# Mixture-of-experts layers of a transformer kernel: ranked groups, each expert fetched once, the smallest group at 64 rows

## The chip, the cores and the metric

The kernel runs on one core of one Trainium2 chip. The metric is the device time of one execution in microseconds. The numbers are fp32: every weight tile is split on the chip into a high part and a low part (both fp32r), and a product x·w is computed as xh·wh + xl·wh + xh·wl, three matmuls for one.

## The reference, cut to what matters

The whole model is four layers over 256 tokens of width 1024. The change touches only the two mixture-of-experts layers, one after each of the first two mixers:

```python
def hier_moe(x, wr_g, br_g, wr_e, br_e, w_gate, w_up, w_down):
    ...
    g_logits = (xt @ wr_g + br_g).astype(f32)
    _, g_idx = lax.top_k(g_logits, 1)                 # 1 of 4 groups for each token
    ...
    top_v, top_i = lax.top_k(e_logits, MOE_TOP_K)     # 2 of that group's 4 experts
    e_w = jax.nn.softmax(top_v, axis=-1) * g_w[:, None]
    ...
        h = jax.nn.silu(xc @ wg) * (xc @ wu)          # 16 experts, 1024 -> 512
        h = (h.reshape(-1, N_EXPERTS, EXPERT_HIDDEN) * gc[..., None])...
        return h @ wd                                 # 512 -> 1024, summed over the experts
```

Each token uses two experts, both of its own group. So 256 tokens fall into four groups, and a group's experts need only the group's tokens.

## The kernel before, in words

Each engine runs its own program, written out in Python in the order in which it is to run; semaphores tie them together (`wait_ge(signal, name)` waits until the instruction that carries that name has ended). The engines in the expert stage (class `Moe`) do this:

- **SP** fetches tiles of 128x1024 fp32 (512 KB) in the order of `MOE_TILES` into a ring of ten (`rawb`, `experts`). A tile's place is fetched anew when its low part has been made.
- **ACT** (`Scalar.split_half`, profile line 522) copies a tile to its high part, **DVE or POOL** (`Low.split_half`, line 549: raw minus high) makes the low part. The field `lo` in `stream_order` says which of the two. There are five places for split tiles; `fed()` stands at the point where a tile has been used and splits the tile that takes its place, so the lead over TensorE is at most five tiles.
- **PE** (matmuls line 608, transposes line 624) works in *units*. A unit is one expert for one block of up to 128 gathered tokens: eight gate-and-up tiles, six matmuls of 512 columns each (`pe_first`); silu on ACT, the product with the gate on DVE (`scalar_tensor_tensor`, line 105), four transposes (`pe_turn`), the transposed h split by ACT and DVE (`hid`); four down tiles, six matmuls each (`pe_down`).

The tokens of each group are gathered to one block with one-hot matmuls (`pe_gather`, matrix `P`): blocks 0 to 3. Tokens beyond 128 in a group go to a fifth block. That makes `UNITS = 19`: 16 units, whose tiles have fixed addresses, and three more for the fifth block, whose experts are chosen at run time (`dve_chosen` writes `S.chosen`, SP reads it with `value_load`, line 483). SP fetches the first ten tiles of a layer before the routing is known. A block's four units add up in PSUM (`yb`), and the block is split and scattered back with one-hot matmuls (`pe_combine`, `pe_place_last`). The order is a fixed pipeline, `steps(UNITS, 2)`: gate-and-up of unit u, then down of unit u-1. POOL makes the low parts of the first four tiles of a layer, DVE all others.

Of the kernel before, what the change touches and what calls it, by code (L numbers as in the profile page):

```python
# [8 lines left out]
F32 = mybir.dt.float32  # L9
# [14 lines left out]
EXPERT_ROOM = 1024 * XRAW + 2560  # L24
# [184 lines left out]
def stream_order(dram):  # L209
# [67 lines left out]
UNITS = 19  # L277
MOE_TILES = [(("gu", "d")[k], u, i) for k, u in steps(UNITS, 2) for i in range((8, 4)[k])]
# [27 lines left out]
class Shared:  # L306


    def __init__(self, nc, ctx, dram, out):
# [6 lines left out]
        self.hrow_ = sb("hrow", 2048)  # L316
        hH = sb("hH", 2048, F32R)
# [14 lines left out]
        self.chosen = sb("chosen", 3, U32)[:, :]  # L332
# [119 lines left out]
class Sync(Lane):  # L452
# [8 lines left out]
    def program(self, S):  # L461
        chosen = None
# [3 lines left out]
        for n, (src, _, lo, ring) in enumerate(S.order):  # L466
            if ring in ("moe0", "moe1") and S.order[n - 1][3] != ring:
                self.wait_ge(S.product, "rows", 2 * int(ring[3]))
                chosen = None
# [6 lines left out]
            if ring in ("moe0", "moe1"):  # L476
                name, layer, unit, k, step = src
                if unit < 16:
                    src = S.dram[name][layer, step * unit + k]
                else:  # L480
                    if chosen is None:
                        self.wait_ge(S.vdone, "moe.chosen", layer)
                        chosen = [self.eng.value_load(S.chosen[0:1, i:i + 1], min_val=0, max_val=15)
                                  for i in range(3)]
                    src = S.dram[name][layer, bass.ds(chosen[unit - 16] * step + k, 1)].rearrange("a p f -> p (a f)")
# [1458 lines left out]
class Moe:  # L1944
# [3 lines left out]
    def __init__(self, S, layer, norm):  # L1948
        self.S, self.layer, self.norm = S, layer, norm
        R = Room(S.experts_r, 2048 * XSPLIT)  # L1950
        self.xr = R.get(5, 2048)
        rows = R.get(2, 2, 1024)
        self.rH, self.rL = rows[:, 0, :, :], rows[:, 1, :, :]
        self.P = R.get(2, 640)
        self.PT = R.get(1280)
        self.tri, self.all, self.hot = self.PT[:, 256:384], self.PT[:, 384:512], self.PT[:, 512:532]
        self.pair = self.PT[:, 544:576].rearrange("p (a g e) -> p a g e", a=2, g=4)
        self.g2 = self.PT[:, 1040:1056].rearrange("p (a f) -> p a f", a=2)
        R = Room(S.experts, 1024 * XRAW)
        self.s = [R.get(512) for _ in range(2)]  # L1960
        self.h = [R.get(512) for _ in range(2)]
# [17 lines left out]
        self.first = R.get(2)  # L1979
        self.e1 = R.get(2, 4)  # L1980
        self.e2 = R.get(2, 4)
        self.seldom_e = R.get(4)
        self.turned = R.get(3)
        self.past = R.get(3)
        self.take = R.get(3, 4)
        self.at = R.get(1)
        self.pos = R.get(2, 4)
        self.over = R.get(2)
        self.full = R.get(5)
# [4 lines left out]
        self.gate = R.get(20)  # L1994
        self.hT = [S.hid[:, 1024 * i:1024 * i + 1024] for i in range(2)]
# [5 lines left out]
    def x_stat(self, b, k):  # L2001
        return self.xr[:, b, 128 * k:128 * k + 128], self.xr[:, b, 1024 + 128 * k:1152 + 128 * k]

    def pe(self, pe):
        S, n = self.S, self.layer
        pe.rows_T = ("hT", self.norm)
        self.pe_route(pe)
        self.pe_count(pe)
        self.pe_gather(pe)
        yb = tb = None  # L2010
        for u in range(UNITS + 1):
            if u == 0:
                for k in range(8):
                    self.pe_first(pe, 0, k, k + 1)
                    if 1 <= k < 5:
                        self.pe_gather_over(pe, (k - 1) // 2 * 4, (k - 1) % 2)
                    elif k == 5:
                        self.pe_gates(pe)
                        self.pe_turn_hot(pe, 0)
                    elif k == 6:  # L2020
                        self.pe_turn_hot(pe, 1)
                        self.pe_turn_hot(pe, 2)
            elif u < UNITS:
                self.pe_first(pe, u, 0, 4)
                self.pe_turn(pe, u - 1, tb)
                self.pe_first(pe, u, 4, 8)
            else:
                self.pe_combine(pe, 1, range(4))
                self.pe_turn(pe, u - 1, tb)
                self.pe_combine(pe, 0, range(4))  # L2030
            if u == 0:
                yb = [pe.open("moe.y", n, i) for i in range(2)]
                tb = [pe.open("moe.T", n, i) for i in range(2)]
            elif u < UNITS:
                self.pe_down(pe, u - 1, yb)
        self.pe_down_last(pe, yb)
        for half in range(2):
            self.pe_place_last(pe, half)
# [28 lines left out]
    def pe_count(self, pe):  # L2067
# [9 lines left out]
        pe.busy(b, 4)  # L2077
# [6 lines left out]
    def pe_gather(self, pe):  # L2084
        S, n = self.S, self.layer
        for k in range(8):
            for part, r in ((0, self.rH), (1, self.rL)):
                b = pe.open("moe.g", n, k, part)
                if k + part == 0:
                    pe.busy(b, 3)  # L2090
                for t in range(2):
# [4 lines left out]
                    ins = pe.mm(b, r[:, t, 128 * k:128 * k + 128], self.P[:, t, 0:512], t == 0, t == 1)  # L2096
                pe.out(ins, ("moe.g", n, k, part))

    def pe_gates(self, pe):
# [3 lines left out]
        pe.wait_ge(S.vdone, "moe.Po", n)  # L2103
        for i in range(5):
            for t in range(2):
                ins = pe.mm(b[:, 8 * i:8 * i + 8], self.P[:, t, 128 * i:128 * i + 128], self.g2[:, t, :],
                            t == 0, t == 1)
        pe.out(ins, ("moe.sg", n))

    def pe_gather_over(self, pe, k0, part):  # L2110
        S, n = self.S, self.layer
        b, r = pe.open("moe.o", n, k0, part), (self.rH, self.rL)[part]
        pe.wait_ge(S.vdone, "moe.Po", n)
        for k in range(4):
            cols = slice(128 * (k0 + k), 128 * (k0 + k) + 128)
            for t in range(2):
                ins = pe.mm(b[:, 128 * k:128 * k + 128], r[:, t, cols], self.P[:, t, 512:640], t == 0, t == 1)
        pe.out(ins, ("moe.o", n, k0, part))

    def pe_turn_hot(self, pe, q):  # L2120
        S, n = self.S, self.layer
        b = pe.open("moe.pt", n, q)
        for i in range(4 * q, min(4 * q + 4, 10)):
            ins = pe.tr(b[:, 128 * (i % 4):128 * (i % 4) + 128],
                        self.P[:, i % 2, 128 * (i // 2):128 * (i // 2) + 128].bitcast(F32))
        pe.out(ins, ("moe.pt", n, q))

    def pe_first(self, pe, u, k0, k1):
        S, n = self.S, self.layer
        G, U = S.accs[2 * (u % 2)], S.accs[2 * (u % 2) + 1]  # L2130
        if u >= 2 and k0 == 0:
            pe.wait_ge(S.vdone, "moe.u", n, u - 2)
        for k in range(k0, k1):
            if u == 0:
                pe.wait_ge(S.acted, "moe.xH", n, k)
                pe.wait_ge(S.vdone, "moe.xL", n, k)
            elif u == 16:
                pe.wait_ge(S.acted, "moe.oH", n, k // 4 * 4)
                pe.wait_ge(S.vdone, "moe.oL", n, k // 4 * 4)
            h, l = pe.high()  # L2140
            xh, xl = self.x_stat(u // 4, k)
            pe.mm(G, xh, h[:, 0:512], k == 0, False)
            pe.mm(U, xh, h[:, 512:1024], k == 0, False)
            pe.mm(G, xl, h[:, 0:512], False, False)
            pe.mm(U, xl, h[:, 512:1024], False, False)
            pe.low()
            pe.mm(G, xh, l[:, 0:512], False, k == 7)
            ins = pe.mm(U, xh, l[:, 512:1024], False, k == 7)
            pe.out(ins, ("half", pe.half), *([("moe.f", n, u)] if k == 7 else []))
            pe.half += 1  # L2150
            pe.tile += 1

    def pe_turn(self, pe, u, tb):
        S, n = self.S, self.layer
        b = tb[u % 2]
        pe.wait_ge(S.vdone, "moe.u", n, u)
        if u >= 2:
            pe.wait_ge(S.vdone, "moe.hl", n, u - 2)
        for j in range(4):
            ins = pe.tr(b[:, 128 * j:128 * j + 128], self.h[u % 2][:, 128 * j:128 * j + 128])  # L2160
        pe.out(ins, ("moe.t", n, u))

    def pe_down(self, pe, u, yb):
        S, n = self.S, self.layer
        hT = self.hT[u % 2]
        if u % 4 == 0 and u:
            pe.wait_ge(S.vdone, "moe.yL", n, u // 4 - 1, 1)
        pe.wait_ge(S.acted, "moe.hh", n, u)
        pe.wait_ge(S.vdone, "moe.hl", n, u)
        for j in range(4):  # L2170
            hh, hl = hT[:, 128 * j:128 * j + 128], hT[:, 512 + 128 * j:640 + 128 * j]
            first, last = u % 4 + j == 0, (u % 4, j) == (3, 3)
            h, l = pe.high()
            for i in range(2):
                pe.mm(yb[i], hh, h[:, 512 * i:512 * i + 512], first, False)
            for i in range(2):
                pe.mm(yb[i], hl, h[:, 512 * i:512 * i + 512], False, False)
            pe.low()
            for i in range(2):
                ins = pe.mm(yb[i], hh, l[:, 512 * i:512 * i + 512], False, last)  # L2180
            pe.out(ins, ("half", pe.half), *([("moe.down", n, u)] if j == 3 else []))
            pe.half += 1
            pe.tile += 1

    def pe_down_last(self, pe, yb):

        S, n, m0 = self.S, self.layer, pe.half
        hT = self.hT[(UNITS - 1) % 2]
        pe.wait_ge(S.acted, "moe.hh", n, UNITS - 1)
        pe.wait_ge(S.vdone, "moe.hl", n, UNITS - 1)  # L2190
        for i in range(2):
            cols = slice(512 * i, 512 * i + 512)
            for j in range(4):
                hh, hl = hT[:, 128 * j:128 * j + 128], hT[:, 512 + 128 * j:640 + 128 * j]
# [1263 lines left out]
```

## Time and profile before

| | before |
|---|---|
| median of 3 runs | 2969.55 us (2968.68 to 2969.96) |
| the profiled execution: span from first to last instruction | 2968.4 us |
| PE, DVE, ACT, POOL busy | 98%, 73%, 61%, 37% of the span |
| expert stage of layer 0 | about 183 to 531 us of the span |
| expert stage of layer 1 | about 740 to 1087 us |

The profile gives the profiled execution's time as its span alone; it lies 1.2 us below the median of the timed runs and 0.3 us below the fastest. Times are microseconds from the span's start. A matmul's recorded duration (about 390 ns for 512 columns) overlaps the next one, so PE's pace is read from the spacing of matmuls, not from their durations.

### The profile page before, as it was taken

The numbers are of one execution on the slowest core, as the hardware profiler recorded it, in microseconds if no ns is written. First come the engines' busy times: TensorE is split into PE (matmuls) and PEld (weight loads), VectorE is DVE, ScalarE is ACT, GpSimd is POOL, SyncE is SP. The second block draws the span as 40 slices with busy tenths as digits, with TensorE's granted clock in tenths as the row PEclk, the third lists the DMA queues.
The fourth block names the chain that finished last, engine by engine and source line by source line (L and its number), as shares of the span: only waits on it lengthen the run. The fifth ranks groups of instructions, "written<-read, shape, count | busy, mean of one in ns | idle before, by whom it ended". The sixth has DMA issues, their size and how long they took to land.

```text
span 2968.4 us, 47605 instructions
## 1 busy us (share of the span) xinstructions
PE 2907.5 (98%) x17290; PEld 2545.4 (86%) x17290; DVE 2171.7 (73%) x4116; ACT 1812.1 (61%) x2954; POOL 1112.6 (37%) x945
## 2 busy tenths in 40 slices
PE   8999999998999999999999999999999999999998
PEld 7778888777888877899999988887799999988887
DVE  4589999245999976596777577776578677577777
ACT  5658887344788865556666555555555666555554
POOL 4520000521100016788777401104578877711010
PEclk9999999999999999999999999999999999999999
DMA  6369999532899953467666777775357666777776
GB/s 234 116 220 368 374 372 359 185 114 96 311 367 373 366 197 123 160 204 219 200 205 202 239 244 238 244 243 187 131 164 226 208 202 205 214 245 242 244 238 206
DMA packets 200536, 689.12 MB, mean 232 GB/s; under 512 B 23218, under 2 KB 24370, under 8 KB 200048
## 3 DMA queue, kind: packets, MB, share of 16 engines
q1 hardware_dynamic: 167184, 606.49, 60.9%
q10 hardware_dynamic: 21056, 40.08, 3.6%
q0 software_dynamic: 12064, 39.52, 3.4%
q8 instruction: 138, 2.26, 0.3%
q14 instruction: 94, 0.77, 0.1%
HBM read 647.19 MB, written 38.80 MB: 231 GB/s over the span
## 4 chain that ended last, share of the span: by engine, by line
PE 93%; DVE 4%; ACT 1%; DMA 1%; issue 1%; POOL 0%; DVEq 0%; SPq 0%; ACTq 0%
PE ps L608 91%; PE ps L624 1%; DVE hrow L105 1%; DVE ps L105 1%; DVE arena L105 0%; DVE arena L95 0%; POOL splitb L549 0%; DMA hrow<-in_x_rows 0%; DVE experts_r L95 0%; DVE hL L95 0%; ACT arena L159 0%; ACT hH L159 0%; ACT splitb L522 0%; ACT experts_r L159 0%; DMA rawb<-in_ab_out 0%
## 5 line engine op out<-in xcount | busy, mean ns | idle before, releaser
L549 POOL TENSOR_TENSOR splitb<-rawb,splitb 128x512 fp32r<-128x512 f32 x744 | 959.7, 1302 | 1052.1 <-ACT splitb L522 1040.6
L522 ACT ACTIVATE splitb<-rawb 128x512 fp32r<-128x512 f32 (+1 forms) x1311 | 828.5, 638 | 734.5 <-PE ps L608 624.4
L608 PE MATMUL ps<-hH,splitb 128*128 128x256 f32 x5248 | 984.7, 284 | 5.2 <-ACT splitb L522 2.3
L608 PEld LDWEIGHTS ps<-hH,splitb 128*128 128x128 f32 x5248 | 834.7, 192 | 12.5 <-issue 8.3
L608 PE MATMUL ps<-splitb,hid 128*128 128x512 f32 x3444 | 788.3, 389 | 0.0
L608 PEld LDWEIGHTS ps<-splitb,hid 128*128 128x128 f32 x3444 | 646.3, 188 | 135.0
L608 PE MATMUL ps<-hL,splitb 128*128 128x256 f32 x2624 | 743.4, 283 | 0.0
L549 DVE TENSOR_TENSOR splitb<-rawb,splitb 128x512 fp32r<-128x512 f32 (+1 forms) x567 | 393.4, 714 | 179.6 <-ACT splitb L522 178.2
L608 PEld LDWEIGHTS ps<-hL,splitb 128*128 128x128 f32 x2624 | 504.2, 192 | 0.4
L608 PE MATMUL ps<-experts_r 128*128 128x512 f32 (+4 forms) x1350 | 320.4, 384 | 2.2 <-DVE experts_r L95 1.3
L608 PEld LDWEIGHTS ps<-experts_r 128*128 128x128 f32 (+1 forms) x1350 | 244.0, 188 | 56.2 <-DVE experts_r L95 4.4
L3231 POOL DMA_DIRECT2D aux<-spill x128 | 69.1, 540 | 592.4 <-DVE hid L95 586.0
L95 DVE TENSOR_TENSOR arena<-ps,arena 128x256 f32<-128x256 f32 (+5 forms) x304 | 130.6, 430 | 205.0 <-ACT arena L159 161.6
L522 ACT ACTIVATE splitb<-experts 128x1024 fp32r<-128x1024 f32 (+1 forms) x201 | 194.3, 974 | 75.1 <-PE ps L608 74.8
L159 ACT ACTIVATE arena<-ps 128x256 f32<-128x256 f32 (+6 forms) x412 | 170.0, 413 | 69.6 <-ACT gb L159 32.2
L549 DVE TENSOR_TENSOR experts_r<-experts,experts_r 128x1024 fp32r<-128x1024 f32 x157 | 190.6, 1224 | 15.9 <-ACT experts_r L522 11.0
L549 DVE TENSOR_TENSOR splitb<-experts,splitb 128x1024 fp32r<-128x1024 f32 x157 | 190.8, 1224 | 14.3 <-ACT splitb L522 11.2
L608 PE MATMUL ps<-splitb,hH 128*128 128x512 f32 x608 | 195.2, 402 | 4.3 <-DVE hL L95 2.2
L608 PE MATMUL ps<-splitb,experts_r 128*128 128x512 f32 x780 | 197.0, 397 | 0.2
L522 ACT ACTIVATE experts_r<-experts 128x1024 fp32r<-128x1024 f32 x161 | 169.3, 1059 | 37.2 <-PE ps L608 36.9
L608 PEld LDWEIGHTS ps<-splitb,experts_r 128*128 128x128 f32 x780 | 144.7, 188 | 34.0 <-POOL splitb L549 1.0
L105 DVE SCALAR_TENSOR_TENSOR aux_r<-ps,aux,aux_r 128x256 fp32r<-128x256 f32 x344 | 149.0, 475 | 0.0
(175 smaller groups left out, 3095.6 us busy)
## 6 DMA issues: line engine op xcount, KB each, us to landing
rawb<-in_peer_u SPq DMA_DIRECT2D x256, 512.0 KB, 3.9
rawb<-in_peer_v SPq DMA_DIRECT2D x256, 512.0 KB, 4.2
experts<-in_moe_gu SPq DMA_DIRECT2D x217, 512.0 KB, 5.5
experts<-in_moe_d SPq DMA_DIRECT2D x105, 512.0 KB, 5.4
rawb<-in_moe_gu SPq DMA_DIRECT2D x87, 512.0 KB, 5.5
aux<-spill POOLq DMA_DIRECT2D x128, 256.0 KB, 4.5
spill<-gb ACTq DMA_DIRECT2D x120, 256.0 KB, 4.1
rawb<-in_moe_d SPq DMA_DIRECT2D x47, 512.0 KB, 5.4
```

Of the source, the lines that this page charges most:

```text
L95: self.eng.tensor_tensor(o, a, b, op).then_inc(self.done.sem, self.done.step(*names))
L105: self.eng.scalar_tensor_tensor(out=o, in0=a, scalar=s, in1=b, op0=op0, op1=op1, accum_out=accum).then_inc(self.done.sem, self.done.step(* ...
L159: self.eng.activation(o, a, f, bias=bias, scale=scale).then_inc(self.done.sem, self.done.step(*names))
L522: self.eng.activation(S.split(m)[0], S.raw(n)[:, off:off + w], ACT.Copy).then_inc(S.hi.sem, S.hi.step(("half", m)))
L549: self.eng.tensor_tensor(l, raw, h.bitcast(F32), ALU.subtract).then_inc(self.low.sem, self.low.step(("half", m), *([("raw", n)] if last el ...
L608: return self.eng.matmul(o, w, x, start=start, stop=stop)
L624: return self.eng.transpose(o, a, self.S.ident)
L3231: pool.eng.dma_start(self.hb[i % 3], S.spill.ap()[n, i, :, :]).then_inc(ring.sem, ring.step(("back", i)))
```

## The change

**Groups are ranked by size** (`rank`), and block b belongs to the group of rank b. Block 0 is the largest group's first 128 tokens; its tokens beyond 128 are placed from the far end of block 1, behind the second group's tokens (the two together have at most 256). The largest group's tokens that use its least used expert are placed first, so that expert needs only block 0. There are 16 units, one for each expert: `parts(u)` is (0, 1) for three of the largest group's experts ("heavy": twelve matmuls a tile), otherwise one block. No expert is fetched twice: 192 tiles a layer for 228.

**The smallest group has at most 64 tokens.** Its stationary operand holds the 64 high columns and the 64 low columns side by side, so a tile takes four matmuls ("light"): both halves times wh, both times wl. The lower and upper 64 rows of the sums are then added (`fold`: two ACT copies, two DVE additions), silu and gate follow in `thin`.

**The order is a written plan** (`moe_plan`): in each round of four units the heavy one, the light one, and two of one block ("medium", six matmuls a tile). A unit's gate and up sums, the transposed h and the down sums use one pair of PSUM banks (`PAIR`). So a unit's result is copied out by ACT right behind its down tiles (`act_sums`), and **POOL adds it** to the block's sum in SBUF (`pool_add`, 14 times a layer) and makes the low parts of the four sums (`pool_low`). POOL also makes **every fifth tile's low part**.

**Every tile's address depends on the routing**: SP waits for `moe.chosen` before the first fetch of a layer.

```diff
-                lo="pool" if i < 4 else "dve")
+                lo="pool" if i < 4 or i % 5 == 4 else "dve")
...
+UNITS = [(r, j) for j in range(4) for r in (0, 3, 2, 1)]
...
+    r, j = UNITS[u]
+    return (0, 1) if r == 0 and j < 3 else (r,)
...
+PAIR = {(0, 0): 0, (0, 1): 2, (1, 3): 1, (2, 2): 3, (3, 1): 0,
...
+        gu(u + 1, *range(8))
+        gu(u + 2, 0, 1)
+        plan.append(("thin", u + 1, 0))
+        gu(u + 2, 2, 3)
+        plan.append(("turn", u, 0))
+        plan.append(("turn", u + 1, 0))
+        gu(u + 2, 4, 5, 6, 7)
+        down(u)
+        down(u + 1)
+        gu(u + 3, 0, 1, 2, 3)
+        plan.append(("turn", u + 2, 0))
+        gu(u + 3, 4, 5, 6, 7)
+        down(u + 2)
...
-                if unit < 16:
-                    src = S.dram[name][layer, step * unit + k]
...
+                if unit not in chosen:
+                    self.wait_ge(S.vdone, "moe.chosen", layer)
+                    at = 4 * UNITS[unit][0] + UNITS[unit][1]
+                    chosen[unit] = self.eng.value_load(S.chosen[0:1, at:at + 1], min_val=0, max_val=15)
...
+        h, l = pe.high()
+        for b in parts(u):
+            (G, U), (xh, xl) = self.banks(u, b), self.x_stat(b, k)
+            pe.mm(G, xh, h[:, 0:512], k == 0, False)
+            pe.mm(U, xh, h[:, 512:1024], k == 0, False)
+            if xl is not None:
+                pe.mm(G, xl, h[:, 0:512], False, False)
+                pe.mm(U, xl, h[:, 512:1024], False, False)
...
+        pool.tt(self.sums[b], self.sums[b], self.part[e % 2], ALU.add, ("moe.add", n, e),
...
+        pool.tt(self.low[b], self.sums[b], self.high[b].bitcast(F32), ALU.subtract, ("moe.yL", n, b))
```

**POOL in layer 0.** Before, it makes four low parts of expert tiles (128x1024) and is idle until the next mixer's tiles (128x512):

```order
L549 TENSOR_TENSOR splitb<-rawb,splitb 128x512 x35
L549 TENSOR_TENSOR splitb<-experts,splitb 128x1024 x2
L549 TENSOR_TENSOR experts_r<-experts,experts_r 128x1024 x2
L549 TENSOR_TENSOR splitb<-rawb,splitb 128x512 x4
```

Now, from the middle of the stage, low parts (line 602, `splitb` and `experts_r` are places for split tiles) and sums (line 95, `y` holds the blocks' sums, `aux` a unit's result) stand among each other:

```order
L602 TENSOR_TENSOR experts_r<-experts,experts_r 128x1024
L95 TENSOR_TENSOR y<-y,aux 128x1024
L602 TENSOR_TENSOR experts_r<-rawb,experts_r 128x1024
L602 TENSOR_TENSOR experts_r<-experts,experts_r 128x1024
L602 TENSOR_TENSOR experts_r<-rawb,experts_r 128x1024
L602 TENSOR_TENSOR experts_r<-experts,experts_r 128x1024
L602 TENSOR_TENSOR experts_r<-rawb,experts_r 128x1024
L95 TENSOR_TENSOR y<-y,aux 128x1024 x2
L602 TENSOR_TENSOR experts_r<-experts,experts_r 128x1024
L95 TENSOR_TENSOR y<-y,aux 128x1024
```

POOL has 60 of these 128x1024 operations in a layer (42 low parts, 14 sums, 4 low parts of sums), for four before.

**DVE behind a unit.** Before, between the product with the gate (line 105) of one unit and that of the next there are twelve low parts and the low part of h (`hid<-ps,hid`):

```order
L105 SCALAR_TENSOR_TENSOR experts<-experts,ps 128x512
L549 TENSOR_TENSOR experts_r<-experts,experts_r 128x1024 x3
L549 TENSOR_TENSOR splitb<-experts,splitb 128x1024 x2
L95 TENSOR_TENSOR hid<-ps,hid 128x512
L549 TENSOR_TENSOR experts_r<-rawb,experts_r 128x1024 x3
L105 SCALAR_TENSOR_TENSOR experts<-experts,ps 128x512
```

Now, in the first round, behind the heavy unit:

```order
L105 SCALAR_TENSOR_TENSOR experts<-experts,ps 128x512 x2
L602 TENSOR_TENSOR experts_r<-experts,experts_r 128x1024 x2
L602 TENSOR_TENSOR splitb<-experts,splitb 128x1024 x2
L602 TENSOR_TENSOR experts_r<-rawb,experts_r 128x1024 x2
L95 TENSOR_TENSOR experts<-ps,experts 64x512 x2
L602 TENSOR_TENSOR splitb<-experts,splitb 128x1024 x2
L602 TENSOR_TENSOR experts_r<-experts,experts_r 128x1024
L105 SCALAR_TENSOR_TENSOR experts<-experts 64x512
L602 TENSOR_TENSOR experts_r<-experts,experts_r 128x1024
L95 TENSOR_TENSOR hid<-ps,hid 128x512 x2
L95 TENSOR_TENSOR experts_r<-ps,experts_r 128x4x64
```

The light unit's last step (`experts<-experts 64x512`, in `thin`) stands behind nine low parts of DVE's from the heavy unit's gate product on, and TensorE's transposes of that unit wait for it.

## Rows read from the trace of the kernel before

**Rows 1.** The page: span, busy times, chain that ended last

```profile
span 2968.4 us, 47605 instructions
PE 2907.5 (98%) x17290; PEld 2545.4 (86%) x17290; DVE 2171.7 (73%) x4116; ACT 1812.1 (61%) x2954; POOL 1112.6 (37%) x945
PE 93%; DVE 4%; ACT 1%; DMA 1%; issue 1%; POOL 0%; DVEq 0%; SPq 0%; ACTq 0%
```

**Rows 2.** Chain that ended last, layer 0's experts: start us, us, what

```profile
209.48 5.80 PE ps L608 x24
215.28 0.44 PE ps L624 x4
215.72 16.58 PE ps L608 x72
```

**Rows 3.** Windows: us, busy of PE, PEld, DVE, ACT, POOL; clock, DMA share, GB/s

```profile
726.00:728.00 2.00, 0.50 (x5) 0.25 (x3) 1.14 (x4) 1.65 (x2) 0.00 (x0) 0.94 1.03 416
728.00:730.00 2.00, 2.00 (x10) 1.47 (x8) 1.86 (x2) 1.44 (x4) 0.00 (x0) 0.50 1.09 436
730.00:732.00 2.00, 2.00 (x9) 1.54 (x8) 1.10 (x4) 2.00 (x4) 0.00 (x0) 0.70 1.01 408
220.00:500.00 280.00, 280.00 (x1251) 228.70 (x1250) 262.32 (x239) 227.53 (x239) 0.00 (x0) 1.00 0.99 370
```

**Rows 4.** Timeline of DVE and ACT, expert stage, POOL idle

```profile
199.08 1.22 DVE L549 TENSOR_TENSOR experts_r<-experts,experts_r 128x1024 fp32r<-128x1024 f32 x1
200.21 2.35 DVE L549 TENSOR_TENSOR splitb<-experts,splitb 128x1024 fp32r<-128x1024 f32 x2
302.75 0.68 DVE L95 TENSOR_TENSOR hid<-ps,hid 128x512 fp32r<-128x512 f32 x1
306.88 2.01 ACT L522 ACTIVATE splitb<-experts 128x1024 fp32r<-128x1024 f32 x2
307.28 0.74 DVE L105 SCALAR_TENSOR_TENSOR experts<-experts,ps 128x512 f32<-128x512 f32 x1
```

**Rows 5.** Timeline of POOL and DVE at the start of layer 0's experts

```profile
190.05 4.74 POOL L549 TENSOR_TENSOR experts_r<-experts,experts_r 128x1024 fp32r<-128x1024 f32 x2
192.73 2.08 DVE L95 TENSOR_TENSOR experts<-experts,cst 128x4 f32<-128x4 f32 x1
195.03 0.16 DVE L95 TENSOR_TENSOR experts<-experts,cst 128x4 f32<-128x4 f32 x1
195.23 0.16 DVE L115 TENSOR_REDUCE experts<-experts 128x1 f32<-128x4 f32 x1
```

**Rows 6.** Timelines of DVE and POOL in the mixers

```profile
140.87 0.69 DVE L95 TENSOR_TENSOR arena<-arena,aux 128x512 f32<-128x512 f32 x1
141.46 6.38 POOL L549 TENSOR_TENSOR splitb<-rawb,splitb 128x512 fp32r<-128x512 f32 x4 [2.68 <-ACT splitb L522]
143.33 1.67 DVE L95 TENSOR_TENSOR arena<-arena,aux 128x512 f32<-128x512 f32 x1
147.51 1.49 DVE L95 TENSOR_TENSOR hL<-ps,hH 128x512 fp32r<-128x512 f32 x2 [0.81 <-ACT hH L159]
2594.05 2.21 DVE L549 TENSOR_TENSOR splitb<-rawb,splitb 128x512 fp32r<-128x512 f32 x2 [6.57 <-ACT splitb L522]
```

**Rows 7.** Stage's start and end; a run-time address on SP; landings in `experts`

```profile
183.31 0.50 PE L608 MATMUL ps<-experts_r 128*128 128x512 f32 x1
191.31 2.96 PE L608 MATMUL ps<-splitb,experts_r 128*128 128x512 f32 x12
529.25 2.31 PE L608 MATMUL ps<-experts_r 128*128 128x512 f32 x8
182.56 1.42 DVE L95 TENSOR_TENSOR experts_r<-cst,experts 128x512 fp32r<-128x512 f32 x2
L483 SPq TENSOR_LOAD <-chosen x3: 270/274/470, 447.8 to 449.2; - x3
DMA to landing us min/median/max: 3.4/5.4/11.2
```

More of the change, by code:

```diff
@@ L2120, in pe_turn_hot @@
[L2120 to L2141, printed above, removed]
+        if k == 0:
+            for b in parts(u):
+                old = self.before_in(u, b)
+                if old is not None:
+                    pe.wait_ge(S.acted, "moe.y", n, *old)
+                elif PAIR[u, b] % 2:
+                    for i in range(2):
+                        pe.open("moe.pb", n, PAIR[u, b] - 1 + i)
@@ L2147, in pe_first @@
+        pe.low()
+        for b in parts(u):
+            (G, U), (xh, xl) = self.banks(u, b), self.x_stat(b, k)
             pe.mm(G, xh, l[:, 0:512], False, k == 7)
             ins = pe.mm(U, xh, l[:, 512:1024], False, k == 7)
[L2149 to L2153, printed above, removed]
+        pe.out(ins, ("half", pe.half), *([("moe.f", n, u)] if k == 7 else []))
+        pe.half += 1
@@ L2154, in pe_turn @@
+        pe.tile += 1
+    def pe_turn(self, pe, u):
         S, n = self.S, self.layer
[L2155 to L2163, printed above, removed]
-        S, n = self.S, self.layer
[L2165 to L2183, printed above, removed]
@@ L2305, in act_turned_hot, with act_silu @@
                ("drained", ("moe.pt", n, q)))
+    def act_silu(self, act, u):
+        S, n = self.S, self.layer
+        act.wait_ge(S.product, "moe.f", n, u)
+        for i, b in enumerate(parts(u)):
+            G, U = self.banks(u, b)
+            if b == 3:
+                act.cp(self.fold[0][0:64, :], G[64:128, :], ("moe.bg", n, u))
+                act.cp(self.fold[1][0:64, :], U[64:128, :], ("moe.bu", n, u))
+            else:
+                act.act(self.s[i], G, ACT.Silu, ("moe.s", n, u, b))
@@ new lines, in act_sums @@
+    def act_sums(self, act, u):
+        S, n, adds = self.S, self.layer, self.adds()
+        act.wait_ge(S.product, "moe.down", n, u)
+        for b in parts(u):
+            to = self.sums[b]
+            if (u, b) in adds:
+                e = adds.index((u, b))
+                to = self.part[e % 2]
+                if e >= 2:
+                    act.wait_ge(S.gdone, "moe.add", n, e - 2)
+            for i in range(2):
+                act.cp(to[:, 512 * i:512 * i + 512], self.banks(u, b)[i],
+                       *([("moe.y", n, u, b)] if i else []),
+                       *([("drained", ("moe.pb", n, 2 + i))] if u == 14 else []))
@@ L2314, in dve, with act_high @@
+    def act_high(self, act, b):
+        S, n = self.S, self.layer
+        if b == 2:
+            act.wait_ge(S.product, "moe.f", n, 15)
+        act.wait_ge(S.gdone, "moe.sum", n, b)
+        act.cp(self.high[b], self.sums[b], ("moe.yH", n, b))
     def dve(self, dve):
```

631 lines of the change are left out of this document (385 added, 246 removed), and 3 rows, old and new, of the table PAIR.

## The prediction

> **What bounds the kernel now.** I read the page first [rows 1]: TensorE (PE) is busy 98% and the chain that ended last is 93% PE. Then the chain inside the expert stage [rows 2]: from 215 us on it is only PE, 72 matmuls in 16.58 us and four transposes in 0.44 us, unit after unit. So one matmul of 512 columns costs 16.58 / 72 = 0.230 us and a unit 17.02 us; nothing else holds it. Third, the windows [rows 3]: from 220 to 500 us the 16 DMA engines have a share of 0.99 at 370 GB/s and DVE is busy 262.3 of 280 us, 94%, with POOL at 0. PE sets the pace, but two others run close behind it, and the change cuts PE's work per tile in places. Before adding its savings I look at what they run into.
>
> **What the change takes off PE, per layer.** Units: 19 x 72 = 1368 matmuls before. After: three heavy units of 144, nine medium of 72 (the largest group's fourth expert, four of rank 1, four of rank 2), four light of 48: 432 + 648 + 192 = 1272. 96 fewer x 0.230 = **-22.1 us**. Transposes: 76 before, 76 after. Scatter: 40 matmuls before and after. Unit 0 starts at 191.31 us [rows 7]; the first transposes behind it stand at 215.28, behind 24 matmuls of unit 1 [rows 2], so unit 1 began at 215.28 - 5.52 = 209.76. Unit 0 took 18.45 us, of which its 48 matmuls are 11.05; the other 7.4 us are the fifth block's 32 gather matmuls, ten for the gates, ten transposes of P and short waits. Eight and eight of the small ones stay, 1.9 us: **-5.5 us**. The sum for PE is -27.6 us a layer. If nothing but PE counted, the kernel would gain 55 us less the next item.
>
> **The start of the layer.** SP may fetch only after `moe.chosen`. DVE's small operations start 0.2 us apart [rows 5]. It has six more of them ahead of the ranks, two more ahead of P, which it now writes in four pieces (+0.3), and the 12 of `dve_chosen` behind it. P is ready at 184.0 before [rows 7]; I get 186.0, and 188.5 for `chosen`. Then come SP's load of the address, 0.27 [rows 7], with what it does behind it and the issue some 0.8 in all, the first landing, 3.4 at its shortest [rows 7], and the high part, 1.0 [rows 4]: 193.8 us. The low part is POOL's, 2.4 [rows 5]: 196.3. PE does its eight high matmuls (1.8 us), waits 0.6, then goes on, as if started at 194.5 instead of 191.3: **+3.2 us**. The gather's narrower matmuls (448 columns) are inside that wait. Then the gates: some seven of DVE's small operations read two SBUF operands while POOL makes the first five low parts, and wait for it (next part); g4 comes near 208 us where PE wants it at about 206.6: **+1.5 us**.
>
> **POOL and DVE share a path: the term that decides.** At the start of layer 0's experts [rows 5] POOL makes two low parts of 128x1024 from 190.05 to 194.79 us. A DVE operation on *four* elements, both inputs in SBUF, starts at 192.73, takes 2.08 us and ends where POOL's ends; the same operation takes 0.16 when POOL is idle. At full size [rows 6], 128x512 with two SBUF inputs takes 0.69 alone and 1.67 beside POOL, and POOL's four of that size then take 1.60 each, where a 128x1024 takes only 2.4 [rows 5]. DVE's `hL<-ps,hH` at 147.51, one input in PSUM, keeps its pace (two in 1.49). At 2594 us two of DVE's low parts beside POOL take 2.21 us. So an operation of either engine that has two SBUF inputs waits until the other engine's has ended, and then runs at full speed; only its first 0.1 us or so is hidden. The Trainium skill (GPSIMD Engine Reference, Key points) says that GpSimd shares its SBUF interfaces with VectorE, with contention for DVE instructions that have two SBUF inputs; it gives no size. The trace agrees and gives the size, a whole operation of 2.4 us.
>
> Every low part of a tile has two SBUF inputs, on DVE and on POOL, and so have POOL's sums. Before, POOL is idle for 19 units. Now the two engines are one queue. Per layer, from 193.8 us on:
> - 150 low parts on DVE at 1.14, the spacing from 199.08 to 200.21 (1.13) and of the pair behind it [rows 4]: 171.0
> - DVE's own: 15 gate products at 0.74, 15 low parts of h at 0.68 [rows 4], 12 operations of 64x512 taken at 0.68 (no row has them; by free size they are the 0.68 row), four of 128x256 at about 0.42: 31.1
> - 60 operations of POOL at 2.4 [rows 5] less the hidden 0.1: 138
>
> Together 340 us. Of DVE's own, 28 us read PSUM and may lie under a POOL operation; POOL fills 138 / 340 = 0.4 of the time: -11. Idle is forced by the five split places: in the heavy units PE takes 2.76 us a tile, the queue needs 0.8 x 1.14 + 0.2 x 2.3 = 1.37, and may be only five tiles ahead. 36 heavy tiles last 99 us; in them lie 36 tiles and six refills of four (82 us) and some four sums (9): +8. +11 more for the thin step's waits (below) and the start. 348 us, so the last low part is made at 542. Behind it PE has half of the last down, one block's scatter and the last one's, 29 matmuls, and two copies, 8 us: **550, where it is 531 now [rows 7]: +19 us a layer**.
>
> A walk through two stretches of a later round gives the same sign. *Light stretch*: at PE's end of the heavy gate-and-up, four tiles are split. Eight light tiles are 7.4 us of PE, eight medium ones 11.0, transposes 1.4: 19.8. DVE must do two gate products (silu first, so to 2.4 us), tiles 5 to 8, two fold additions, eight medium tiles less one, then `thin`, with two or three POOL tiles between: that is near 18 us. But PE wants `thin` behind its fourth medium tile, at 14. It waits there some 4 us. *Down stretch*: PE needs 20.7 us for four light, eight and four medium tiles. POOL gets two sums at once and a third soon after (7 us) among three of its low parts; the 16 tiles and the sums take 16 x 1.37 + 7 + 2 own = 31, less the lead of four tiles: +5 to +7. Light stretches then cost 3 x 4 + 10 (in the last round the first unit is medium, so there is no lead to start with), down stretches 2 x 7, 1 in the first round (no sums yet) and 10 in the last: 47, and 4.7 at the start. 52 - 27.6 = **+24 us a layer**.
>
> I take 23, between the two and nearer the walk, which knows the order of waits; 46 for both layers: 2968.4 + 46 = 3014, and with the 1.2 us by which the median lies above the span, **3016 us**.
>
> **Edits at nothing.** ACT: 192 high parts near 1.0 us [rows 4], plus some 50 us of copies and silus, is 250 in 350. The aux load goes to the stage's end; the mixer's first use of it is over 14 us behind the stage. Banks: a pair is opened again behind ACT's two copies (1.2 us), while PE has four light tiles (3.7 us) in front; without that cover it would be 1.2 us a round.
>
> **Rivals.**
> - *PE's sum shows* (other side). The ring of five and POOL's idle moments hide the queue, and only 4.7 us of the start and about 4 us of latency a layer are lost: -27.6 + 8.7 = -19, both layers -38: **2931**. For it: PE's savings are certain, and 312 us (340 with every PSUM-reading operation under POOL) would end at 514, below 531. It decides from the point where DVE's waits for POOL stay under about 40 us a layer. Against it: before, DVE is busy 94% in a steady order and still wants a low part almost always.
> - *The queue packs half-way*: **2975**, +3 us a layer; about no change.
> - *The clock falls in the waits*: PE was busy 0.50 of 2 us at 726 and the next 4 us ran at a granted clock of 0.50 and 0.70 [rows 3], the lower level of 1.2 GHz for part of it. Eight waits a layer at 1.7 us each put 27 us on top: **3043**.
> - *Transfers bind.* 416 GB/s and more were moved in the windows from 726 us on [rows 3], 1.26 us a tile; a light tile is 0.92 us of PE, but an average one 1.57, and ten places cover the difference: **2937**. By the Trainium skill (DMA: Bandwidth & Descriptors, Specifications) HBM gives a core about 358 GB/s, an estimate of 1.46 us a tile, and the units of a last round would wait for it; the trace shows faster transfers than that.
>
> **How the numbers follow.** Forecast 0.57 (its own range 2990 to 3040), half-way 0.15, PE's sum 0.20, clock 0.05, transfers 0.03. The bound of a visible change is 0.2%, 5.9 us, about what a measurement of this kernel can tell. Faster: 0.20 + 0.03 + a third of half-way, 0.28; same 0.06; slower 0.66. The range goes from PE's sum, 2930, to 3050.
>
> **What would show it.** Right: in the expert stage DVE's low parts have a mean well above 1.22 us (about 1.8), with long ones ending at a POOL operation's end; PE waits for DVE or POOL (lines 602, 95), longest before the 64-row transposes; a layer's stage lasts near 370 us. Heavy units run at 0.230 us a matmul. Wrong: DVE's low parts stay at 1.22 beside POOL, or POOL's work falls where DVE waits for PE anyway; then PE's busy share stays above 97% and the stage lasts near 330.

## The result and the profile after

The changed kernel takes 3053.4 us (median of 4 runs, 3052.4 to 3055.3), the kernel before 2969.8 (4 runs, 2968.7 to 2974.4): ratio 1.0279, 95% interval 1.0264 to 1.0293. It is slower by 84 us; the forecast had +46. The sign and the shared path were forecast, the size was not, and the time lies 3 us above the range.

The page of the changed kernel, as in [rows 1]:

```profile
span 3053.6 us, 47728 instructions
PE 2905.5 (95%) x17050; PEld 2520.4 (83%) x17050; DVE 2157.8 (71%) x3990; ACT 1772.6 (58%) x2956; POOL 1434.6 (47%) x1057
PE 78%; DVE 13%; ACT 3%; issue 2%; DMA 1%; POOL 1%; ACTq 0%; DVEq 0%; SPq 0%; POOLq 0%
```

Read the last line against [rows 1]: PE's share of the chain that ended last falls from 93% to 78%, and DVE's rises from 4% to 13%. PE is idle 87 us more (148.1 for 60.9). It executes 240 matmuls fewer and yet is busy for about the same time; in part that is its clock, of which the mean granted over the span falls from 0.997 to 0.985.

Layer 0's stage (first matmul of the gather, last of the scatter), as in [rows 7]:

```profile
187.08 0.47 PE L661 MATMUL ps<-experts_r 128*128 128x448 f32 x1
573.13 2.02 PE L661 MATMUL ps<-experts_r 128*128 128x512 f32 x8
```

It ends at 575 us where it ended at 531.6: 43.6 of the 85 us are in layer 0. The windows of the stage, with the columns of [rows 3]:

```profile
220.00:300.00 80.00, 74.19 (x326) 58.61 (x325) 61.30 (x48) 55.81 (x65) 24.41 (x9) 1.00 0.82 287
300.00:380.00 80.00, 70.81 (x300) 55.22 (x299) 62.79 (x46) 54.30 (x64) 36.77 (x13) 0.98 0.79 275
380.00:460.00 80.00, 71.05 (x297) 56.22 (x296) 57.91 (x41) 49.45 (x57) 37.66 (x13) 0.94 0.73 249
460.00:540.00 80.00, 68.00 (x272) 52.13 (x270) 72.38 (x47) 58.55 (x66) 40.63 (x15) 0.91 0.86 299
```

PE was busy 280 of 280 us in [rows 3]; now it lacks 6, 9, 9 and 12 of 80. The DMA share has fallen from 0.99 to about 0.8, so transfers don't bind. DVE makes 41 to 48 operations in a window, and before it made 239 in 280 us, 68 in 80. Why is in the groups of DVE and POOL, by form, from 186 to 600 us:

```profile
L602 DVE TENSOR_TENSOR splitb<-experts,splitb 128x1024 fp32r<-128x1024 f32 x76 | 129.3, 1726 | 48.9 <-ACT splitb L575 48.7
L602 DVE TENSOR_TENSOR experts_r<-rawb,experts_r 128x1024 fp32r<-128x1024 f32 x38 | 64.3, 1712 | 7.7 <-ACT experts_r L575 7.7
L602 DVE TENSOR_TENSOR experts_r<-experts,experts_r 128x1024 fp32r<-128x1024 f32 x36 | 64.3, 1807 | 6.7 <-ACT experts_r L575 6.6
L602 POOL TENSOR_TENSOR experts_r<-experts,experts_r 128x1024 fp32r<-128x1024 f32 x21 | 60.4, 2880 | 94.3 <-ACT experts_r L575 94.3
L95 POOL TENSOR_TENSOR y<-y,aux 128x1024 f32<-128x1024 f32 x14 | 41.3, 2948 | 22.0 <-ACT aux L159 21.7
```

DVE's low part has a mean of 1.72 us for the 1.22 of [rows 4], and POOL's 2.88 for 2.4. The timeline shows what the means hide:

```profile
548.79 6.51 DVE L602 TENSOR_TENSOR splitb<-experts,splitb 128x1024 fp32r<-128x1024 f32 x2 [1.96 <-ACT splitb L575]
551.02 3.20 POOL L95 TENSOR_TENSOR hL<-y,experts_r 128x1024 fp32r<-128x1024 f32 x1
554.18 3.36 POOL L602 TENSOR_TENSOR experts_r<-rawb,experts_r 128x1024 fp32r<-128x1024 f32 x1
555.22 3.41 DVE L602 TENSOR_TENSOR experts_r<-rawb,experts_r 128x1024 fp32r<-128x1024 f32 x1
558.68 0.73 PE L661 MATMUL ps<-experts_r,hid 128*128 128x512 f32 x2 [1.67 <-DVE experts_r L602]
```

Each engine's record covers its own work and the rest of the other's ahead of it: POOL 3.36 = 2.3 + 1.1, DVE 3.41 = 1.1 + 2.3. While both have work they take turns, and two operations come out in 3.4 us. The DVE operation that began at 555.22 ends at 558.63, and PE, which waited 1.67 us for it, goes on at 558.68.

PE's waits from 195 to 560 us (who waits, for whom: total us, times, longest; PEld is PE's weight load, which runs ahead of its matmul); before, from 195 to 520 us, no row of this kind was above 0.8:

```profile
PEld ps L661 <- DVE experts_r L602: 21.7, 14, 2.6
PEld ps L661 <- POOL experts_r L602: 10.3, 6, 5.0
PEld ps L2262 <- DVE experts L105: 8.8, 4, 2.9
PEld ps L661 <- DVE splitb L602: 6.7, 10, 2.1
PE ps L661 <- DVE hid L95: 6.0, 3, 4.4
```

Line 2262 is the light unit's 64-row transposes, which wait for the thin step. The three rows of weight loads that wait for low parts add up to 38.7 us. Matmuls were still running for part of that: the same three waits in rows of matmuls are 16.1, 7.8 and 3.3, together 27.2 us, and that at line 2262 is 7.9.

### The profile page after: what moved, and what is told of

Read it like the earlier page. It is cut to its first block, busy times and chain, and to the rows that moved or that the text cites. A ratio compares the mean times of both kernels' runs of the same rounds, so it can differ in the third digit from the quotient of the medians.

```text
span 3053.6 us, 47728 instructions
## 1 busy us (share of the span) xinstructions
PE 2905.5 (95%) x17050; PEld 2520.4 (83%) x17050; DVE 2157.8 (71%) x3990; ACT 1772.6 (58%) x2956; POOL 1434.6 (47%) x1057
## 4 chain that ended last, share of the span: by engine, by line
PE 78%; DVE 13%; ACT 3%; issue 2%; DMA 1%; POOL 1%; ACTq 0%; DVEq 0%; SPq 0%; POOLq 0%
PE ps L661 77%; DVE experts_r L602 4%; DVE splitb L602 3%; DVE hrow L105 1%; ACT splitb L575 1%; PE ps L677 1%; POOL splitb L602 1%; DVE experts L95 1%; ACT experts_r L575 1%; DMA rawb<-in_peer_u 1%; DVE ps L105 1%; DVE arena L95 1%; DVE arena L105 0%; DVE experts L105 0%; DVE experts_r L100 0%
## 5 line engine op out<-in xcount | busy, mean ns | idle before, releaser
L575 ACT ACTIVATE splitb<-rawb 128x512 fp32r<-128x512 f32 x1284 | 801.8, 630 | 729.3 <-PE ps L661 620.1
L661 PE MATMUL ps<-splitb,hid 128*128 128x512 f32 x3384 | 776.2, 390 | 2.7 <-DVE splitb L602 1.7
L661 PEld LDWEIGHTS ps<-splitb,hid 128*128 128x128 f32 x3384 | 637.5, 189 | 137.9 <-DVE splitb L602 2.4
L602 DVE TENSOR_TENSOR splitb<-rawb,splitb 128x512 fp32r<-128x512 f32 x544 | 365.0, 692 | 177.8 <-ACT splitb L575 177.2
L661 PEld LDWEIGHTS ps<-experts_r 128*128 128x128 f32 (+1 forms) x1250 | 233.8, 193 | 116.2 <-DVE experts_r L602 39.1
L602 DVE TENSOR_TENSOR splitb<-experts,splitb 128x1024 fp32r<-128x1024 f32 x152 | 257.9, 1722 | 99.5 <-ACT splitb L575 99.3
L661 PE MATMUL ps<-splitb,experts_r 128*128 128x512 f32 x780 | 207.1, 413 | 4.2 <-DVE splitb L602 2.2
L602 POOL TENSOR_TENSOR experts_r<-experts,experts_r 128x1024 fp32r<-128x1024 f32 x42 | 120.4, 2871 | 185.3 <-ACT experts_r L575 185.3
L602 POOL TENSOR_TENSOR experts_r<-rawb,experts_r 128x1024 fp32r<-128x1024 f32 x38 | 108.7, 2860 | 155.8 <-ACT experts_r L575 155.8
L575 ACT ACTIVATE experts_r<-rawb 128x1024 fp32r<-128x1024 f32 x114 | 118.4, 1055 | 77.8 <-PE ps L661 77.5
```

The costliest lines, as they stand in the source:

```text
L575: self.eng.activation(S.split(m)[0], S.raw(n)[:, off:off + w], ACT.Copy).then_inc(S.hi.sem, S.hi.step(("half", m)))
L602: self.eng.tensor_tensor(l, raw, h.bitcast(F32), ALU.subtract).then_inc(self.low.sem, self.low.step(("half", m), *([("raw", n)] if last el ...
L661: return self.eng.matmul(o, w, x, start=start, stop=stop)
```

## The experiments

All 15 were compared with the kernel before on the same chip. "+/-" is against the changed kernel's 3053.4 unless another run is named.

**e1: POOL makes only the first four low parts of a layer.** 

> The changed kernel, but POOL makes no low part of a tile behind the first four of a layer (DVE makes all 188 others); POOL keeps its 18 operations on sums. Shared path: DVE's queue is 188 x 1.14 + 31 + 22 x 2.3 = 296 us a layer for 340, so up to 44 us a layer come back, until PE is the bound again: 2983, between 2960 and 3010, and DVE's low parts have a mean near 1.25. Rival, the plan itself costs the time (thin step, banks, sums, start) and POOL's help is a relief: DVE gets 38 more operations of 1.14 us a layer, up to 43 us more, 3060 to 3120. Rival, clock: if lost clock is a share of its own, the time comes back only in part, and the granted clock in the windows of the stage stays under 0.95.

```diff
-                lo="pool" if i < 4 or i % 5 == 4 else "dve")
+                lo="pool" if i < 4 else "dve")
```

3012.7 us, -40.7 (ratio to before 1.0139, 1.0123 to 1.0156). Taking 38 helpers' operations a layer away, and giving DVE 38 more, makes the kernel faster; the rival had it slower. But less comes back than the 70 us forecast: 20 a layer, about half of 38 x (2.3 - 1.14) = 44. PE's wait at line 2262 does not go away; it grows from 8.8 to 12.5 us.

**e2: two in five on POOL.** 

> The changed kernel, but POOL makes two of five low parts. Shared path: some 37 operations a layer move from 1.14 to 2.3 us of the one queue, +43 us a layer, nearly all of it seen, since the stage is already paced by the queue: 3125, between 3095 and 3150. Rival, no shared path (DVE's own load is what delays): DVE is relieved of 37 x 1.8 us, POOL has 97 x 2.4 = 233 us in a stage of 387: the time falls, 2990 to 3050.

```diff
+                lo="pool" if i < 4 or i % 5 in (2, 4) else "dve")
```

3107.5 us, +54.1 (1.0458, 1.044 to 1.0475). Again the direction of the shared path, and again less than its full price, 27 a layer for 43. DVE's largest group, in the same view:

```profile
L602 DVE TENSOR_TENSOR splitb<-experts,splitb 128x1024 fp32r<-128x1024 f32 x76 | 175.6, 2333 | 49.6 <-ACT splitb L575 49.5
```

DVE made 37 low parts a layer fewer (113 for 150), and the busy time of its low parts did not fall: 264.9 us for 257.9.

**e3: nearly all work on low parts left out.** 

> The changed kernel, with every low part of an expert tile (but each expert's first gate-and-up and first down tile) made over 64 columns for 1024, so that nearly all work on low parts is left out; PE, ACT, transfers, the plan and the 18 sums on POOL stay. If low parts in the shared queue are the whole loss, what is left is PE's sum with the start: 2925 to 2950. If the plan costs time by itself (thin step, banks, sums, a fallen clock), it stays above 2970.

```diff
+        k = 64 if type(S.order[n][0]) is tuple and w == 1024 and S.order[n][0][2] >= 1 else w
+        self.eng.tensor_tensor(l[:, 0:k], raw[:, 0:k], h[:, 0:k].bitcast(F32), ALU.subtract)...
```

2948.5 us, -105.0. With them gone, the kernel is 22 us faster than the one before, so the loss hangs on the low parts. (PE's clock comes back with them, to a mean of 0.994; the run does not separate the two.) What is left is 17 us above the 2931 of PE's sum: at the edge of what was expected, and taken up by e15.

**e4: the kernel before, with the one line.** 

> The kernel before, with the one line of the change on POOL: every fifth low part of an expert tile on POOL, nothing else. Shared path: 182 low parts on DVE x 1.14 = 207, DVE's own 27, 46 on POOL x 2.3 = 106: 340 us for PE's 323, less what lies under operations that read PSUM (about 7): +5 to +20 us a layer, 2979 to 3010. Rival, no shared path: DVE falls from 94% to 76% busy in the stage and PE stays the bound: 2969, same.

2982.3 us against 2970.8: +11.6 (1.0031, 1.0018 to 1.0044), at the low end of the range, 6 a layer. PE, plan and units are those of before; only help was added. POOL's and DVE's groups:

```profile
L549 POOL TENSOR_TENSOR experts_r<-experts,experts_r 128x1024 fp32r<-128x1024 f32 x25 | 71.8, 2878 | 96.0 <-ACT experts_r L522 96.0
L549 DVE TENSOR_TENSOR splitb<-experts,splitb 128x1024 fp32r<-128x1024 f32 x90 | 159.1, 1799 | 17.5 <-ACT splitb L522 16.8
```

**e5: four small operations ahead of POOL's first low part.** 

> The changed kernel, with the first four operations of dve_gates (two differences for the softmax and the two copies of P for which TensorE's second group of transposes waits) moved ahead of the eight copies of the gathered tokens, where POOL is still idle. In the changed kernel these four take 9.1 us at the start of layer 0, each up to a POOL operation's end; there they cost 0.9. Shared path: PE gets its transposes some 4 us earlier but then waits for the gates, since the small operations behind them still take turns with POOL's first five low parts: -2 to -5 us a layer, 3046, between 3040 and 3051. Rival, the four waits alone are the loss at the start: -8 a layer, 3037. Rival, nothing at the start is on the path: 3053.

```diff
         self.dve_chosen(dve)
+        (two differences, two copies of P, from the head of dve_gates)
         for k in range(8):
```

3052.7 us, -0.7 and not told from nothing; the stage of layer 0 ends 1.8 us earlier. The third theory holds: the start's waits are visible (below), but the time is spent again behind them.

**e6: the light unit's transposes four tiles later.** 

> The changed kernel, with the light unit's transposes behind the last four gate-and-up tiles of the next unit instead of ahead of them, so that nobody waits for the thin step. In the changed kernel PE waits 8.8 us a layer there, in four places. If these waits are a loss of their own, 7 to 9 us a layer come back: 3037. If the queue of DVE and POOL paces these stretches anyway, a part comes back as waits for low parts: 3046, between 3040 and 3053 (this I take). Rival: the light unit's h is now late for its down tiles: 3053 to 3065.

```diff
         plan.append(("turn", u, 0))
-        plan.append(("turn", u + 1, 0))
         gu(u + 2, 4, 5, 6, 7)
+        plan.append(("turn", u + 1, 0))
```

3041.7 us, -11.7: between the two theories. The wait for the thin step at line 2262 (8.8 us) is gone; the waits for low parts grow from 38.7 to 41.5 (same view):

```profile
PEld ps L661 <- DVE experts_r L602: 21.0, 15, 2.5
PEld ps L661 <- POOL experts_r L602: 11.8, 7, 5.0
PEld ps L661 <- DVE splitb L602: 8.7, 10, 2.1
```

**e7: e1, and DVE adds the sums from PSUM.** 

> As e1 (POOL makes only the first four low parts of tiles), and DVE adds a unit's result to the block's sum straight from PSUM (28 operations of 128x512 with one input in PSUM), so ACT's 28 copies and POOL's 14 sums go. Shared path: the queue loses 14 x 2.3 = 32 us a layer and gets 28 x 0.69 = 19 back, 13 less; 24 for both layers from 3013: 2992, between 2980 and 3010. Rival, DVE's load alone counts: +19 a layer, 3040 to 3055.

```diff
+            for i in range(2):
+                cols = slice(512 * i, 512 * i + 512)
+                dve.tt(self.sums[b][:, cols], self.banks(u, b)[i], self.sums[b][:, cols], ALU.add, ...
```

2999.8 us, -13.0 to e1, where 21 were expected. DVE has 28 operations a layer more (0.69 us each, one input in PSUM) and the kernel is faster; the rival of a loaded DVE is out. ACT's 28 copies go too, so the 13 us are not POOL's sums alone.

**e8: e7 with e5 and e6. e9: e7 with e6 alone.** 

> e7 with the edits of e5 and e6 together. DVE waits for POOL only at a layer's start and end. From 2992: the light unit's transposes waited 12.5 us a layer in e1, of which I take 8; 3 from the start: 2970, between 2955 and 2990. If it stays above 2990, the rest of the loss is neither the shared path nor the thin step, but DVE's own pace against light tiles.

 

> e7 with the light unit's transposes moved (the edit of e6), without the early copies of e5; e8 has both. In e7 PE waits 12.6 us a layer ahead of the four light units' transposes. If the order of the thin step is the cost, about 23 us of the 35 between e7 and e8 come from it: 2977, between 2970 and 2985, and the early copies are worth 12. If it is the copies, this run stays near 2990.

2965.1 us (0.9978, 0.9968 to 0.9988) and 2967.3 us (0.9989, 0.998 to 0.9998). The turn's place is worth 32 us here, where 23 were expected, and the early copies 2, for 12 expected. With the shared path and the late thin step gone, the changed kernel is as fast as the one before or slightly faster. DVE's low parts are back at the pace of [rows 4] in e8:

```profile
L602 DVE TENSOR_TENSOR splitb<-experts,splitb 128x1024 fp32r<-128x1024 f32 x76 | 92.3, 1239 | 14.5 <-ACT splitb L575 14.4
```

**e10: matmuls in the wait ahead of the light unit's transposes.** 

> The changed kernel, with eight matmuls of 256 columns (0.24 us each, their sums are not used) on PE ahead of each light unit's transposes, where it waits some 2.2 us for the thin step. They begin when the fold addition has read the bank. Clock theory: the granted clock in layer 0 is 0.83 to 0.96 in seven windows of 20 us, 14 us of lost clock in all; if the waits ahead of the transposes cause the fall, the clock comes back and 5 to 20 us of the time: 3040. Queue theory: DVE and POOL pace these stretches and a slow PE hides behind them: 3053, between 3048 and 3058.

```diff
+            if b == 3:
+                pe.wait_ge(S.vdone, "moe.ag", n, u)
+                pe.busy(o, 8)
             pe.wait_ge(S.vdone, "moe.u", n, u, b)
```

3054.9 us, +1.5: the queue's theory. Two windows of the changed kernel, and the same of e10:

```profile
420.00:440.00 20.00, 17.87 (x78) 14.45 (x77) 16.01 (x15) 11.13 (x14) 7.65 (x2) 0.91 0.89 310
440.00:460.00 20.00, 15.37 (x59) 12.00 (x58) 13.74 (x7) 12.33 (x15) 13.95 (x5) 0.83 0.53 175
```

```profile
420.00:440.00 20.00, 20.00 (x95) 16.38 (x93) 14.56 (x14) 10.44 (x12) 7.36 (x2) 1.00 0.89 314
440.00:460.00 20.00, 15.36 (x60) 12.12 (x59) 15.32 (x7) 13.31 (x17) 14.73 (x5) 0.83 0.50 177
```

From 420 us on, where PE is now busy 20.00 of 20, the granted clock is 1.00 for 0.91, and no time is gained by it. From 440 us, where PE waits for low parts as before, it stays at 0.83, a mean of the two levels.

**e11: e8, with light tiles between heavy ones.** 

> e8 with the light unit's first four gate-and-up tiles set between the heavy unit's last four (2.76 and 0.92 us of PE in turn). In e8 a light tile (0.92 us of PE) is shorter than DVE's 1.14 and ACT's 1.05 for its parts, and PE still waits in the last rounds. If this pace against light tiles is what is left between e8 and the run without most low parts (2948), half of it and more comes back: 2955, between 2948 and 2962. Rival: the light unit's banks are taken earlier, so PE waits for the sums of the round before: 2966 to 2980.

```diff
                 elif k == 3:
                     down(u - 1)
+                if k >= 4:
+                    gu(u + 1, k - 4)
```

2958.7 us (0.996, 0.9945 to 0.9975), -6.4 to e8. This version is faster than both kernels. 10 us were expected.

**e12: e8 with the change's line on POOL back.** 

> e8 (sums on DVE from PSUM, light unit's transposes late, copies early) with the one line of the change back: every fifth low part on POOL, 38 a layer. It asks whether that line alone turns the mended plan from faster to slower. By e1, 38 of them cost 20 us a layer in the plan of the change; by the queue 38 x (2.3 - 1.14) = 44 less the slack that e8 has (PE 38 us a layer above DVE's 270). So 2965 + 30 = 2995, between 2980 and 3015. If POOL's help costs nothing in a plan without the late thin step: 2965.

3010.3 us (1.0134, 1.0117 to 1.015), +45.2 to e8. The one line turns a plan that gains slightly into one that loses. 30 were expected; the time is inside the range.

**e13: four places for split tiles. e14: six, for two raw places.** 

> The changed kernel, with four places for split tiles of the experts for five, so the lead over PE is four tiles. In the changed kernel, in layer 0 from 196 to 565 us, DVE and POOL have work in 335 us and neither has any in 34. If the missing idle time comes from the short lead (the two run out of places behind heavy units and are late behind light ones), one place less adds 10 to 20 us of it a layer: 3085, between 3070 and 3105. If the queue's own work is all that counts: 3053 to 3060.

 

> The changed kernel, with six places for split tiles for five, paid with two of the ten places for raw tiles. Lead theory: 5 to 12 us of idle a layer come back: 3036, between 3025 and 3046. Rival, queue's work alone: 3053. Rival, eight places for raw tiles let transfers bind: above 3056.

```diff
-            ring = base if name == "base" else wide
+            ring = base if name == "base" else wide[:4]
```

```diff
-XRAW = 7
-XSPLIT = 3
+XRAW = 5
+XSPLIT = 4
```

3051.7 us (-1.7) and 3062.3 us (+8.9). The lead theory expected a longer time from e13 and a shorter one from e14; neither came. e14 changes two things, since it has two raw places fewer as well. The wait ahead of the light unit's transposes, of the changed kernel 8.8, is in e13:

```profile
PEld ps L2262 <- DVE experts L105: 4.5, 4, 1.5
```

and in e14:

```profile
PEld ps L2262 <- DVE experts L105: 17.0, 4, 5.4
```

A longer lead puts one more low part ahead of the thin step in DVE's order (16 for 15 in the first round, 14 in e13), so PE waits for that step longer; a shorter lead gives this back and loses elsewhere, where the weight loads' waits for low parts grow from 38.7 to 44.9. Transfers were late by little in e14: ACT waited 5.0 us for them, 1.3 in the changed kernel.

**e15: e12 with nearly all work on low parts left out.** 

> e12 with low parts of tiles over 64 columns for 1024 (most work on low parts left out, as in e3): PE's floor for the mended plan. e3 stood at 2948 where the forecast had 2931 for PE's sum. If the 17 us of difference are the start's four waits for POOL and the thin step, it comes to 2935, between 2928 and 2942; if they are elsewhere (first fetch, scatter, small waits), it stays at 2943 to 2950.

2935.3 us, -13.1 to e3. It differs from e3 by three edits: the late turn, the early copies and the sums on DVE. Together they give back 13 of the 17 us by which e3 missed PE's sum; which of them gives how much was not run.

## Why the prediction was right in sign and too low in size

**PE's terms** (-27.6 a layer) fit. With most work on low parts left out, the late thin step mended and the copies early (e15), the kernel takes 2935 where the prediction had 2931 for "PE's sum shows"; the term was not measured by itself.

**The start of the layer** was 3 us too short. POOL's first low part begins at 196.60, where the prediction had the first high part ready at 193.8. And PE's second group of transposes of P, which the prediction did not name, waits for two of these four DVE operations:

```profile
196.60 4.73 POOL L602 TENSOR_TENSOR splitb<-experts,splitb 128x1024 fp32r<-128x1024 f32 x2 [38.86 <-ACT splitb L575]
196.91 4.44 DVE L95 TENSOR_TENSOR experts<-experts 128x8 f32<-128x8 f32 x2
201.28 7.04 POOL L602 TENSOR_TENSOR experts_r<-experts,experts_r 128x1024 fp32r<-128x1024 f32 x3
201.39 4.66 DVE L100 TENSOR_SCALAR experts_r<-cst,experts 128x64 fp32r<-128x64 f32 x2
206.20 0.84 PE L677 MATMUL ps<-cst,experts_r 128*128 128x128 f32 x4 [2.71 <-DVE experts_r L100]
```

In e5 these four ran early, and the time stayed (-0.7): this cost nothing in the end.

**DVE and POOL share a path**: right, in kind and in the price of one operation. e1, e2 and e7 went the way of the shared path against a rival with the other sign, e4 and e12 against one with no change. The Trainium skill (Trainium Architecture — The Big Picture, What this means for kernel authors) calls the pair's sharing an exclusive lock and not a split of bandwidth; the alternation of 3.4 us each agrees.

**The queue of 340 us less 11 overlap** was near. Adding up the trace's intervals from 196 to 565 us (369 us; the last low part ends at 564.9), in which either engine has an instruction running, gives 335 us (DVE 297, POOL 168, the overlap counted once), where the forecast was 329.

**The idle of the queue is the step that failed, and in it one term.** The prediction had +8 us, "forced by the five split places" behind heavy units, and +11 for the thin step's waits and the start: 19. The same count gives 369 - 335 = 34 in which neither engine has work. Each idle stretch ends with an operation. Where that is the low part of tile n, its place came free when PE was done with tile n-5. Set down to that tile, 23 us of the idle stand behind tiles of heavy units (12 gate-and-up, 11 down) and 11 elsewhere, and PE was busy in all of it but 0.1. So the 11 came out in its size, and the 8 measured 23. One such stretch, the down tiles of the third round's heavy unit:

```profile
432.31 5.64 PE L661 MATMUL ps<-splitb,hid 128*128 128x512 f32 x24
437.79 5.77 PE L661 MATMUL ps<-experts_r,hid 128*128 128x512 f32 x24
439.14 1.22 DVE L602 TENSOR_TENSOR splitb<-experts,splitb 128x1024 fp32r<-128x1024 f32 x1 [1.50 <-ACT splitb L575]
441.95 1.22 DVE L602 TENSOR_TENSOR experts_r<-rawb,experts_r 128x1024 fp32r<-128x1024 f32 x1 [1.59 <-ACT experts_r L575]
444.75 1.23 DVE L602 TENSOR_TENSOR experts_r<-rawb,experts_r 128x1024 fp32r<-128x1024 f32 x1 [1.57 <-ACT experts_r L575]
```

PE works without a pause at 2.76 us a tile; ACT splits a tile only when PE frees a place, DVE makes its low part in 1.22, and then the queue stands for 1.6. The prediction let the queue fill up six times, four tiles each, while heavy tiles ran. In this stretch they were full when it began. With 15 us more idle, the later start (3), the longer queue (6) and small items, layer 0's stage ends at 575 for 550.

Why the places are full is shown in part. Four tiles ahead of a heavy unit's down tiles PE stands at the light unit's transposes, until DVE has made the low parts in front of the thin step and the step itself; in that wait the lead can fill up. e6 takes this wait away: the idle behind heavy down tiles falls from 11 to 7 us, and the whole of it from 34 to 29. In e9 against e7 the first falls from 17 to 9. The 12 us behind heavy gate-and-up tiles stay at 12 in e6, and for them no run shows why. One place more or less does not change it: behind heavy tiles it is 26 us with four (e13) and 25 with six (e14).

**The walk through two stretches** had the light stretch at 4 us of waiting for `thin`, three times, and 10 in the last round. Measured are 8.8 in all four. The down stretches, where it had PE wait for low parts, made 25 of its 47 us. Waits for low parts are 38.7 us in rows of weight loads and 27.2 in rows of matmuls, so they are the larger part, and the longest wait, 5.0, is for a low part of POOL's and not, as was forecast, ahead of the transposes (2.9).

**Rivals.** *PE's sum shows* and *half-way*: out, since low parts cost 105 us with the plan as it is (e3). POOL's share in that is e1 and e7 together, 54 us. *The clock falls in the waits*: it does, to 0.83 to 0.91 in five of the sixteen windows of 20 us from 220 to 540 us, 13.8 us of lost clock in layer 0 if each window's lack is added. The prediction had 27 for both layers, so its size was near. In e10 3.6 us of it came back and the time did not. So in those stretches it hides behind the queue; whether the rest of it costs anything stays open, and it may be a part of what the next paragraph puts down to low parts. *Transfers bind*: out, share 0.73 to 0.86.

How the 84 us split: PE's floor -35 (e15 against the kernel before), thin step, start and POOL's sums without low parts +13 (e3 against e15), low parts in the shared queue +105 (the changed kernel against e3). Of the last, every fifth tile on POOL is 41 (e1); of the 64 that e1 still has above e3, POOL's sums are 13 (e7) and the thin step's place most of the rest (32 in e9, which may hold a part of the 13 of e3, so these don't add up exactly). Even with POOL out and the thin step mended, low parts cost 30 us (e8 against e15). One likely reason is that DVE's 1.14 us a tile and ACT's 1.05 are longer than a light tile's 0.92 us of PE; e11, which sets light tiles between heavy ones, takes 6 of it back.

## What to carry to other kernels

Before giving POOL a share of DVE's work, look for operations of both with two inputs in SBUF: they form one queue, so a slower helper (2.3 us for 1.14) lengthens it, even when the helper was idle and DVE was 94% busy (e4). Move work to where one input is in PSUM instead (e7). And before lengthening a lead, ask which small step stands behind it in the same engine's order: with one split place more (and two raw places fewer) the wait there went from 8.8 to 17.0 us (e14).

## What the runs showed of the hardware

- Two engines that both have work with two SBUF inputs take turns, operation by operation: at 554 us 3.36 us for POOL's 2.4 us operation, 3.41 for DVE's 1.22.
- DVE's `TENSOR_SCALAR` with one input in SBUF and a column of scalars there (128x64, 0.28 us for the 128x128 form when POOL was idle in e1) takes 2.3 us beside POOL at 201 us. The prediction had counted only operations with two SBUF inputs.
- Operations that read one input from PSUM kept their time in the changed kernel: a mean of 0.681 us for the low part of h and 0.741 for the gate product, as in [rows 4].
